# Next unit's first score matmuls ahead of the row-sum matmuls, at each boundary between attention units

## What is computed

```python
def gqa_attention(q, k, v):                       # A: 8 query heads, 2 key heads, width 64
    s = jnp.einsum('bkgqd,bksd->bkgqs', qb, k) * scale
    p = jax.nn.softmax(s, axis=-1)
    return jnp.einsum('bkgqs,bksd->bkgqd', p, v)

def diff_attention(q, k, v, lam):                 # B: 4 heads, two score maps of width 32 each
    a = jax.nn.softmax(s1, axis=-1) - lam32 * jax.nn.softmax(s2, axis=-1)
    return jnp.einsum('bhqs,bhsd->bhqd', a, v)
```

## Time and profile before

| | |
|---|---|
| median of 3 runs | 2391.35 us (2389.95 to 2392.23) |
| the profiled execution: its own time | 2391.01 us |
| its span, first to last instruction | 2389.1 us |
| TensorE matmuls busy | 2116.7 us, 89% of the span |
| VectorE busy | 1361.4 us, 57% |
| ScalarE busy | 852.0 us, 36% |
| GpSimd busy | 978.2 us, 41% |

### The profile page before, as it was taken

How to read it: one execution, slowest core, us unless ns; L and a number is a source line. 1 busy time by engine, 2 the same in 40 slices (tenths; PEclk the granted TensorE clock), 3 DMA queues, 4 the chain that set the end, 5 groups by cost and what they waited for, 6 DMA issues and landing times. The chain is left out here.

```text
span 2389.1 us, 28515 instructions
## 1 busy us (share of the span) xinstructions
PE 2116.7 (89%) x10517; PEld 1478.5 (62%) x10517; DVE 1361.4 (57%) x2278; ACT 852.0 (36%) x1740; POOL 978.2 (41%) x522
## 2 busy tenths in 40 slices
PE   3799999889999999949938999998899999999498
PEld 1678888655555555528716789885555555555286
DVE  1667200596666666776516672005966666767764
ACT  2432221424445444432124322214244454444321
POOL 0211111325777777760002111113257777777500
PEclk9999999798999999969969999998999999999699
DMA  7332221110001010033373322211100010000333
GB/s 268 114 111 89 62 73 58 36 42 7 19 19 32 19 19 19 7 106 106 100 270 102 115 85 62 73 60 33 42 7 19 19 32 19 19 19 7 106 106 106
DMA packets 188756, 155.74 MB, mean 65 GB/s; under 512 B 125180, under 2 KB 150208, under 8 KB 186560
## 3 DMA queue, kind: packets, MB, share of 16 engines
q1 hardware_dynamic: 185424, 153.35, 21.2%
q10 hardware_dynamic: 3184, 0.47, 0.1%
HBM read 115.37 MB, written 38.42 MB: 64 GB/s over the span
## 5 line engine op out<-in xcount | busy, mean ns | idle before, releaser
L1150 POOL TENSOR_TENSOR prob_sums<-prob_sums,probs 128x1024 f32<-128x1024 f32 x256 | 614.4, 2400 | 108.9 <-ACT probs L1306 83.4
L1306 ACT ACTIVATE probs<-scores 128x512 f32<-128x512 f32 x672 | 361.5, 604 | 437.3 <-PE scores L1208 241.3
L501 POOL TENSOR_TENSOR w_lo<-w_stage,w_hi 128x512 fp32r<-128x512 f32 (+1 forms) x112 | 134.4, 1232 | 818.3 <-ACT w_hi L436 818.3
L1372 DVE TENSOR_REDUCE neg_max_parts<-work 128x1 f32<-128x512 f32 (+1 forms) x640 | 394.2, 683 | 60.5 <-PE work L1188 56.2
L403 PE MATMUL z_acc<-w_hi,h_hi 128*128 128x512 f32 (+1 forms) x640 | 237.0, 370 | 12.0 <-DVE h_lo L520 8.5
L403 PE MATMUL z_acc<-w_hi,h_lo 128*128 128x512 f32 (+1 forms) x640 | 234.2, 366 | 0.0
L403 PE MATMUL z_acc<-w_lo,h_hi 128*128 128x512 f32 (+1 forms) x640 | 234.0, 366 | 0.0
L1404 DVE RECIPROCAL recip_sums<-work 128x512 f32<-128x512 f32 x32 | 107.4, 3358 | 212.1 <-PE work L1240 212.1
L825 DVE MEMSET k_stackB<- 128x24 f32 (+1 forms) x4 | 0.9, 218 | 346.6 <-PEq L287 346.6
L403 PE MATMUL z_acc<-h_hi,w_lo 128*128 128x512 f32 (+1 forms) x528 | 187.0, 354 | 0.0
L403 PE MATMUL z_acc<-h_hi,w_hi 128*128 128x512 f32 (+1 forms) x528 | 186.9, 354 | 0.0
(11 more groups left out here) (230 smaller groups left out, 3734.8 us busy)
## 6 DMA issues: line engine op xcount, KB each, us to landing
w_stage<-in_w_in SPq DMA_DIRECT2D x96, 256.0 KB, 3.1
mod_w<-in_w_mod SPq DMA_DIRECT2D x16, 1024.0 KB, 14.1
z_scratch<-z_out SPq DMA_DIRECT2D x60, 256.0 KB, 2.0
cv<-u_scratch SPq DMA_DIRECT2D x20, 512.0 KB, 6.3
mod_w<-in_w_mod SPq DMA_DIRECT2D x16, 512.0 KB, 21.2
u_scratch<-z_out SPq DMA_DIRECT2D x32, 256.0 KB, 2.0
out_y_sample<-y_tiles SPq DMA_DIRECT2D x16, 512.0 KB, 5.1
q_rawA<-z_scratch SPq DMA_DIRECT2D x16, 320.0 KB, 4.0
```

What stands on the lines that cost most here:

```text
L501: pool.tensor_tensor(w_lo[:, n % RING, 0:cols], stage[:, n % STAGES, 0:cols], w_hi[:, n % RING, 0:cols].bitcast(F32), ALU.subtract).then_i ...
L1150: ins = pool.tensor_tensor(a, a, pr[:, n % NPB, :], ALU.add)
L1306: act.activation(pr[:, n % NPB, c * NB:(c + 1) * NB], sc[m % SCORE_BANKS][:, :], ACT.Exp, scale=SCALE[u]).then_inc(s["a_exp"], 1)
L1372: dve.tensor_reduce(dst, src, AX_X, ALU.max, negate=True).then_inc(s["a_wkdve"], 1)
```

## The change

At each of the 15 boundaries of a layer the scores of step 0 of the next unit are issued ahead of `sums` instead of behind it. Those of step 1 stay behind it. No instruction is added or taken away.

```diff
                 pieces(nxt, PREP_LAST, PREP - PREP_LAST)
                 weigh(p, LAST)
+                if nxt < UNITS:
+                    ahead(nxt, GROUPS[0][0])
                 sums(p)
                 if nxt < UNITS:
-                    for i in GROUPS[0]:
-                        ahead(nxt, i)
+                    ahead(nxt, GROUPS[0][1])
```

## The result

The changed kernel takes 2408.06 us in the median of 6 runs (2400.45 to 2410.25), against 2391.79 us before (2389.95 to 2394.41, 6 runs). The ratio is 1.0059, 95% interval 1.0048 to 1.0069 (the two medians alone give 1.0068): it is slower. The forecast was 2392.4 with a range of 2385 to 2398.5.

What follows compares the result with a forecast made beforehand. TensorE leads, but VectorE's chain sets the start of B and GpSimd its end. Per layer +4.62 - 0.66 - 3.45 = +0.51, two layers +1.0 on 2391.01 us, plus 0.34 to the median: 2392.4, range 2385 to 2398.5.

Steps and rivals of the forecast that it cites:

- A to B: Boundary from even unit (A) to odd (B), 14 times: `sums` and B's first `weigh` come 0.66 us later, +4.62 a layer.
- Scores in between: Price of scores put between `weigh` and `sums`: 0.66 us for two B matmuls, 1.13 us for four A matmuls.
- A to B after unit 6: Twice: two scores fit into the 1.30 us wait for GpSimd, and the later wait for ScalarE goes: -0.66 us each.
- B to A: Boundary from odd unit to even, 14 times: fewer scores behind `sums`, piece 3 held by the reciprocal; gain 0.54 or 0.43 us.
- The sum: All boundaries: +4.62 - 0.66 - 3.45 = +0.51 us a layer, +1.0 for two layers; chance 0.70.
- B to A gives nothing back: Rival: inserted scores take 0.54 us longer at odd-to-even boundaries, so no gain there; +7.9 us, 2399.3, chance 0.15.
- The made-good start: Rival: the late start of B is made good within B, so the 4.62 falls away; -8.2 us, 2384.2, chance 0.12.
- Both gaps closed: Rival: TensorE's waits at both kinds of boundary are all won; 25.8 us faster, 2365.6, chance 0.03.

Runs made afterwards that it cites:

- three traces of this order: The changed kernel (2408.06 us), the same kernel once more (2406.89), and it with each score chunk of step 0 waiting only for its own query copy (2406.66).
- the wait filled: Changed kernel with the last query piece's two transposes repeated four times more ahead of B's first values, in 12 units: 2396.93 us.
- run with work left out: Kernel before, with seven of ten query transposes omitted when units 2, 4, 6, 10, 12 and 14 are prepared: 2400.85 us.
- B to A alone: Kernel before, with the scores of step 0 ahead of `sums` only at boundaries from odd to even units: 2385.39 us.
- A to B only: Kernel before, with the scores of step 0 ahead of `sums` only at boundaries from even to odd units: 2407.85 us.
- before filled: Kernel before, with the last query piece's two transposes repeated twice more ahead of B's first values: 2392.78 us.
- the two with half of B to A: Kernel before, one score chunk ahead of `sums` after odd units, both after unit 6: 2380.22 us; with chunk-wise query-copy waits as well: 2380.84.
- half dose: Kernel before, with one score chunk (one matmul) of step 0 ahead of `sums` only at boundaries from even to odd units: 2401.59 us.

## Why the prediction was wrong

**The step that failed** is the sentence on A to B that TensorE "reaches the first `weigh` earlier, but both then wait: TensorE's wait grows from 0.70 to about 1.6 us", with only +0.66 as its cost. The wait did grow, to 1.68. It was costed at nothing because it lies in front of an instruction that VectorE releases anyway. The runs show that it is not free: the granted clock, 1.00 in the rows, was taken as given. With the wait filled again the changed kernel lost no clock and took 2396.93, inside the range. Without the filling it takes 2406 to 2408: 10 to 11 us are the falls, and 6 to 8 falls of 1.3 to 1.7 us (the long ones 2.55) are seen in the three traces of this order. The traces add up. From the last `weigh` of unit 0 to that of unit 13, both layers together, it is 785.1 us before, 788.9 with the wait filled, and 798.7, 802.3 and 801.5 in the three traces without filling. The B units with a fall are 9.7, 13.2 and 12.5 us longer there than before; without that, each of the three stands at 789.0 to 789.1. The run with work left out shows the same without any instruction moved.

The Trainium skill ("TensorE: Matmul & The Clock Gate", Part 1, on the HAM clock gate) says that TensorE's clock is full or halved by how busy the engine has been of late. The traces agree as far as they go: no fall at the 12 places with waits of 0.79 us or less, 2 to 8 with 1.14 or more. The same part of the Trainium skill says that one kernel has more or fewer matmuls at the low clock from run to run, by the phase at its start. The traces agree in that the changed kernel fell at 6 places in one execution and at 7, partly others, in the next. The Trainium skill's advice there ("Why this matters for your kernels") warns of idle gaps longer than the 1.68 us here, so by that advice alone no fall would have been expected; the measurement decides.

Point by point:

- *Scores in between, 0.66 and 1.13 us.* Mis-sized. The pair of scores itself takes 0.66 (582.65 to 583.31), but the first score comes 1.01 behind the last `weigh`, where `sums` came 0.91 behind it, and the steps from `sums` on take 6.06 instead of 6.00: 0.82 in all. What the 0.10 is stays open; it is not the query copy.
- *A to B after unit 6, -0.66.* Mis-sized: the gain is larger. From the last `weigh` of unit 6 to the first of unit 7 it is 771.69 - 762.30 = 9.39 before and 775.44 - 766.98 = 8.46 after: -0.93. The wait for ScalarE vanished, and the one for the reciprocal at piece 3 stayed, as said:

```profile
766.98 1.08 PE L1224 MATMUL att_out<-probs,vA 128*64 128x512 f32 x4
...
773.71 0.66 PE L1177 MATMUL work<-ident_r,q_stackA 128*128 128x128 f32 x4 [1.03 <-DVE recip_sums L1405]
...
775.44 1.94 PE L1224 MATMUL att_out<-probs,vB 128*64 128x512 f32 x8
```

- *B to A, -0.54 or -0.43.* The mechanism was right (piece 3 is held by the reciprocal, 0.05 us behind its end). But `sums` came 0.30 and not 0.21 later against the last `weigh` (614.28 - 612.15 = 2.13, against 1.83). From the last `weigh` of a B unit to that of the A unit behind it: 641.66 - 609.49 = 32.17 before, 643.95 - 612.15 = 31.80 after, -0.37; where the wait was 0.81, -0.26.
- *The sum.* With the measured terms a layer is 7 x 0.82 - 0.93 - (4 x 0.37 + 3 x 0.26) = +2.55, two layers +5.1. The filled kernel shows +5.0. The forecast of +1.0 was twice the difference of two terms of some 4 us, each off by a fifth to a third; this alone would have left the time in the range.
- *The rivals.* None of them was the cause. The slower one (B to A gives nothing back) is refuted, as B to A alone is a gain. Its time of 2399.3 lies nearest to the measured one, but by another mechanism. The made-good start is refuted by the B units without a fall: unit 3 of layer 1 takes 21.31 us from first to last `weigh`, against 21.34 before. (Its time, 2384.2, is also mis-added: -8.2 on the median of 2391.35 is 2383.1.) Both gaps closed needed an earlier start of B, which did not come.

**What stays open.** The time outside attention moves by some microseconds from one execution to the next: the last `weigh` of unit 0 starts at 581.6 in the changed kernel's first trace, at 583.2 with B to A only and at 585.3 with A to B only, with the same code ahead of it. This hides how much of the +16 of A to B alone is falls; its one trace shows 2, which with an order cost of 14 x 0.82 - 2 x 0.93 = 9.6 us makes 12.3. Also open is what decides between a fall and none: 1.68 us gave 6, 8 and 7 of 12 in the changed order but 2 of 12 with A to B only, 1.27 us gave 2 and 1.14 us gave 7 of 12. The wait that the row prints is thus not the measure by itself. In none of the six kernels with 0.79 us or less (before, B to A only, filled, before filled, and the two with half of B to A) is there a fall at these places. Unit 15, left out of the 12, is no clearer: ahead of its first `weigh` TensorE waits 1.31 to 1.33 us in six of the kernels, and the clock falls there in both layers of three (the two with half of B to A, and the one with transposes left out), while in the other three, before among them, it falls 7.7 to 8.8 us later. From that first `weigh` to `sums` it is 29.5 us in all six: where GpSimd sets the end, the fall cost nothing.

## What to carry to other kernels

A wait of the leading engine that another engine ends is not free space: making it longer can cost the clock of what comes behind it, and the trace of before, at full clock at all 12 places, gives no price for that. Put early work into a wait only as far as it fits: the same move, cut to the size of each wait, took 11.7 us off where the full one added 16. And where a forecast is the small difference of two large terms, size each at its own place, since the spacing of the same instructions in mid-unit was 0.1 us off here, 28 times.

## What was not expected of the hardware

Removing 84 matmuls without moving any made the kernel before 9 us slower, and adding 96 made the changed one 11 us faster. In the stretch of a fall eight rows took 3.45 us instead of 1.87. What TensorE did in the 7 us ahead of the first `weigh` does not sort the places either. These are unit 1 before, then units 1 and 7 of the changed kernel, with the columns of the stretches above:

```profile
581.27:588.27 7.00, 6.00 (x28) 3.14 (x28) 4.84 (x4) 4.90 (x11) 2.64 (x2) 1.00 0.34 55
```

```profile
582.37:589.37 7.00, 5.01 (x25) 2.77 (x23) 4.85 (x4) 4.19 (x9) 3.12 (x2) 0.99 0.35 56
768.44:775.44 7.00, 5.51 (x34) 4.01 (x32) 5.06 (x4) 5.72 (x12) 3.54 (x3) 1.00 0.61 111
```

The first had no fall and the second had one. With 5.5 to 5.6 us, 7 of 12 places fell where transposes were left out, 2 of 12 with the half dose, and unit 7 in none of the seven traces in which it stands at that.
